# Stick-breaking attention: the second sigmoid written into the SBUF row, the scan in place

## The chip, the cores and the metric

The kernel runs on one core of one Trainium2 chip. The time is that of the whole program on the device, in microseconds; a run gives one number. The kernel before was timed three times: 2722.66 us in the median, 2720.82 and 2723.33 at the ends. The engines are named as in the profile: PE is TensorE (PEld its weight loads), DVE is VectorE, ACT is ScalarE, POOL is GpSimd, SP is SyncE.

## The reference, cut to what matters

The program is a trunk of a gMLP layer, a dense MLP, a stick-breaking attention layer and another dense MLP, all on 1024 tokens of width 1024. The change lies in the attention alone: 16 heads of 64, blocks of 128 queries against all keys up to the block.

```python
z = jnp.einsum('bthd,bshd->bhts', qb, kb).astype(jnp.float32) * scale
log_keep = jnp.where(causal, jax.nn.log_sigmoid(-z), 0.0)
survive = lax.cumsum(log_keep, axis=log_keep.ndim - 1, reverse=True) - log_keep
log_a = jax.nn.log_sigmoid(z) + survive
a = jnp.where(causal, jnp.exp(log_a), 0.0)
outs.append(jnp.einsum('bhts,bshd->bthd', a.astype(vb.dtype), vb))
```

The kernel doesn't go through logarithms. For each row it forms the break b = sigmoid(z) and the keep 1 - b = sigmoid(-z), a running product of the keeps from the right (the "stick"), and a = b times the stick of the key to the right.

## The kernel before, in words

Attention works on tiles: one head, one block of 128 queries, all keys up to it. A head has 8 tiles (`NT`), numbered by `tile_of(k)`, with 128 to 1024 keys. They come in pairs `m` in the order 0, 1, 3, 2, so that the widths of a head's tiles are, in order, 128, 256, 384, 512, 896, 1024, 640, 768. The parity `e` of a tile picks one of two score buffers `z_ps[e]`, each two banks of PSUM. A tile goes through these steps:

- PE, `scores` (lines 1218 and 1220): the scores into `z_ps[e]`, the causal mask added by a last matmul. Before the first of them PE waits for the tile two before, which used the same buffer: `stick_done`.
- ACT, `break_tile` (1608): sigmoid(z) from PSUM into the SBUF row `brk[m][e]`.
- ACT, `keep_tile` (1614): sigmoid(-z), from `z_ps[e]` into `z_ps[e]`, counted by `keep_done`.
- DVE, `sticks` (2084): one scan from right to left, from `z_ps[e]` into the SBUF row `stick[m][e]`, counted by `stick_done`. A scan instruction takes two tensors; the second one is not used in the arithmetic (`ALU.bypass`), and `brk[m][e]` stands in its place.
- POOL, `stick_mult` (894): `brk` times `stick`, both in SBUF, back into `brk`, counted by `a_done`.
- PE, `to_keys` (1235): transposes of `brk`; it waits for `a_done` of both tiles of a pair. ACT (1622) copies them to SBUF as `aT`, and PE, `values` (1248), multiplies with v. ACT (1629) and DVE (2091) split the result in a high and a low part.

Each engine's queue is in order, written out by hand and the same for each head. On PE the scores run two pairs ahead: in step n stand `scores` of tile 2n+4, then the first group of transposes of pair n, a group of `values` of pair n-1, `scores` of tile 2n+5, and the other groups. So the scores of the tile of 640 keys, then of 768 keys, then of 128 keys (of the next head) stand in the queue ahead of the first transposes of the pair of 896 and 1024 keys (line 1235), and the scores of the tile of 256 keys behind them. On ACT the two sigmoids stand between the copies of `aT`. On DVE the scans stand one behind another, with line 2091 once every second pair. POOL has the products alone, and twice in the first two heads a weight split (`w_lo`, line 791, two instructions) between them.

Most of the attention is a hardware loop over two heads. The rest of the program (gMLP, both MLPs, projections) is bound by PE, with high and low parts of fp32 operands split by ACT, DVE and POOL.

Of the kernel before, what the change touches and what calls it, by code (L numbers as in the profile page):

```python
# [22 lines left out]
P = 128  # L23
D = 1024
TOK = 1024
NT = TOK // P
# [144 lines left out]
def wait(eng, sem, value):  # L171

    if isinstance(value, int) and value <= 0:
        return
    eng.wait_ge(sem, value)
# [56 lines left out]
def tile_of(k):  # L232

    m, e = pair(k // 2), k % 2
    return (k // NT) % 2, m, e, 2 * m + e


def build(nc, x, g_mix_pre, g_mix_post, g_ffn_pre, g_ffn_post, w_in, v_g, v_b, w_s, b_s, w_aout,
          w_qkv, w_bout, w1, w2, out):
    ctx = ExitStack()  # L240
    with ctx:
        def sem(name):
            return ctx.enter_context(nc.semaphore(name))
# [4 lines left out]
        def at(name, shape, dt, offset=None):  # L248
            size = 4 if dt != BF16 else 2
            for s in shape[1:]:  # L250
                size *= s
            if offset is None:
                offset = place[0]
                place[0] += -(-size // 32) * 32
                assert place[0] <= 229344, (name, place[0])
            return nc.alloc_sbuf_tensor_at(name, shape, dt, offset=offset)
# [3 lines left out]
        def kb(name, shape, dt, k):  # L260
# [21 lines left out]
                for e in range(2)] for m in range(QP)]  # L282
# [21 lines left out]
        stick = [[at(f"stick{m}{e}", [P, (2 * m + 2) * P + 8], F32, o_stick[m] + e * ((m + 1) * 1024 + 32))  # L304
                  for e in range(2)] for m in range(QP)]
# [50 lines left out]
        z_ps = [psum[:, 2 * b:2 * b + 2, :].rearrange("p a n -> p (a n)") for b in range(2)]  # L356
# [60 lines left out]
        keep_done = sem("keep_done")  # L417
        brk_done = sem("brk_done")
        rows_set = sem("rows_set")
        stick_done = sem("stick_done")  # L420
        a_done = sem("a_done")
# [491 lines left out]
        def _(pe):  # L913
# [293 lines left out]
            def scores(i, k):  # L1207

                hb, _, zb, tb = tile_of(k)
                if tb == 0:  # L1210
                    pe.wait_ge(qk_in[hb], (i + k // (2 * NT)) * (6 * 16) + 6 * 16)
                wait(pe, stick_done, i * (2 * NT) + (k - 1))
                s = (tb + 1) * P
                for c0 in range(0, s, HALF):

                    c1 = c0 + max(2 * P, min(HALF, s - c0))
                    for n in range(2):
                        mm = pe.matmul(z_ps[zb][:, c0:c1], q_st[hb][:, tb * P:(tb + 1) * P], k_st[hb][n][:, c0:c1],  # L1218
                                       start=(n == 0), stop=(n == 1 and c1 < s))
                mm = pe.matmul(z_ps[zb][:, s - P:s], ident_bf[:], mask_bf[:], start=False, stop=True)  # L1220
                mm.then_inc(z_done, 1)
# [31 lines left out]
            def att_step(i):  # L1253
                first, last = isinstance(i, int) and i == 0, isinstance(i, int) and i == HEADS // 2 - 1
                if first:
                    for k in range(4):
                        scores(0, k)
                    pe.wait_ge(rows_set, 2)
                for n in range(2 * QP):
                    more = not (last and n >= 2 * QP - 2)  # L1260
                    if more:
                        scores(i, 2 * n + 4)

                    here = pair(n) + 1
                    before = 0 if first and n == 0 else pair(n - 1) + 1
                    for g in range(max(here, before)):
                        if g < here:
                            to_keys(i, n, g)
                        if g < before:
                            if n:  # L1270
                                values(i, n - 1, g)
                            else:
                                values(i - 1, 2 * QP - 1, g)
                        if more and g == 0:
                            scores(i, 2 * n + 5)
# [25 lines left out]
        def _(act):  # L1301
# [309 lines left out]
            def keep_tile(i, k):  # L1611
                _, m, e, tb = tile_of(k)
                act.wait_ge(brk_done, i * (2 * NT) + (k + 1))
                act.activation(z_ps[e][:, 0:(tb + 1) * P], z_ps[e][:, 0:(tb + 1) * P],  # L1614
                               ACT.Sigmoid, scale=-SCALE).then_inc(keep_done, 1)

            def keys_in(i, n, g):
# [14 lines left out]
            def att_step(i):  # L1632
                first, last = isinstance(i, int) and i == 0, isinstance(i, int) and i == HEADS // 2 - 1
                if first:
                    for k in range(4):
                        break_tile(0, k)
                        keep_tile(0, k)
                    act.wait_ge(qk_out[1], 32 * (2 * D // UC) // 2)
                for n in range(2 * QP):

                    out = None if n % 2 == 0 or (first and n == 1) else (i, n // 2 - 1) if n > 1 else (i - 1, 3)
                    for g in range(4):
                        if not (last and n >= 2 * QP - 2):
                            (break_tile if g % 2 == 0 else keep_tile)(i, 2 * n + 4 + g // 2)
                        if g <= pair(n):
                            keys_in(i, n, g)
                    if out:
                        out_hi(*out)
                    if first and n in (2, 4):
                        hi(U_O + n // 2 - 1, n // 2 - 1)  # L1650
# [13 lines left out]
        def _(dve):  # L1664
# [411 lines left out]
            def sticks(i, k):  # L2076

                _, m, e, tb = tile_of(k)
                dve.wait_ge(keep_done, i * (2 * NT) + (k + 1))
                wait(dve, a_done, i * (2 * NT) + (k - NT + 1))  # L2080
                row = stick[m][e][:, (1 - e) * P:(2 * m + 2) * P][:, ::-1]
                unused = brk[m][e][:, (1 - e) * P:(2 * m + 2) * P]
                keep = z_ps[e][:, 0:(tb + 1) * P][:, ::-1]
                dve.tensor_tensor_scan(row, keep, unused, 1.0, ALU.mult, ALU.bypass).then_inc(stick_done, 1)  # L2084

            def out_lo(i, r):
                h2, g = r // 2, r % 2
# [6 lines left out]
            def att_step(i):  # L2094
                first, last = isinstance(i, int) and i == 0, isinstance(i, int) and i == HEADS // 2 - 1
                if first:
                    for k in range(4):
                        sticks(0, k)
                    dve.wait_ge(qk_out[1], 32 * (2 * D // UC) // 2)
                    ones_column(QP - 1)  # L2100
                    dve.wait_ge(rows_set, 2 + 2 * QP)
                for n in range(2 * QP):
                    more = not (last and n >= 2 * QP - 2)
                    out = None if n % 2 == 0 or (first and n == 1) else (i, n // 2 - 1) if n > 1 else (i - 1, 3)
                    for g in range(4):
                        if more and g % 2 == 0:
                            sticks(i, 2 * n + 4 + g // 2)
                    if out:
                        out_lo(*out)
# [44 lines left out]
```

## Time and profile before

| | |
|---|---|
| median of three runs | 2722.66 us |
| the profiled execution | 2723.14 us |
| its span, first to last instruction | 2721.4 us |
| PE busy over the span | 2543.8 us, 93% |
| DVE, ACT, POOL busy | 1482.9, 1028.4, 1113.1 us |
| mean granted TensorE clock | 0.977 of full speed |
| attention | about 1577 to 1940 us of the span |
| DVE scans, line 2084 | 128, 173.4 us |
| POOL products, line 894 | 128, 153.4 us |

A row of the timeline is: start in us from the span's start, duration in us, engine, line, operation, output<-inputs by the program's names, shape, how many instructions are merged in it, and in brackets the idle time of the engine just before it with what ended it. Where two instructions are merged, the duration is that of both together. Tiles are told apart by their width: 128x896 is the tile of 896 keys. `psum` is both the score buffers and the transposes. A wait is told as "who line <- what it waited for: us in total, times, longest". A row of the windows gives the busy time of each engine in one stretch, the mean granted TensorE clock (1.00 is full speed), and the share of the DMA engines.

### The profile page before, as it was taken

The page shows a single profiled execution, that of the slowest core. Times are in us where ns is not written, and L with a number is a line of the kernel's source. Part 1 is how long each engine was busy: PE and PEld are TensorE (multiplying, and loading weights), DVE is VectorE, ACT ScalarE, POOL GpSimd, SP SyncE. Part 2 cuts the span into 40 slices and gives each one's busy share as a digit, 9 for nine tenths or more (in the row PEclk, how much of TensorE's full clock was granted, in tenths as well). Part 3 has the DMA queues.
Part 4 walks back from the last instruction along what each step waited for, and adds up shares of the span by engine and source line. Part 5 has one row for each costly group of instructions (what it writes and reads, how often), then busy time and mean ns, then how long its engine had stood idle before and what let it go on. Part 6 is the DMA issues. An engine that isn't in the chain of part 4 may idle for free.

```text
span 2721.4 us, 35430 instructions
## 1 busy us (share of the span) xinstructions
PE 2543.8 (93%) x13100; PEld 2152.2 (79%) x13100; DVE 1482.9 (54%) x1959; ACT 1028.4 (38%) x1507; POOL 1113.1 (41%) x716
## 2 busy tenths in 40 slices
PE   7998999998999989999899978888997999989997
PEld 7997888876888868887898857776896888768886
DVE  3214655657656577776311135555348655577775
ACT  5222212234444333334211157777335444333332
POOL 2221221136555465554222144444235555465554
PEclk9999999998999989999999989999999999989999
DMA  5222121142544464443224544334122544464443
GB/s 163 93 92 93 63 70 54 62 133 77 169 151 157 141 229 149 157 171 124 94 93 155 185 116 109 92 92 100 47 80 95 171 151 147 163 231 139 139 166 120
DMA packets 180417, 342.56 MB, mean 126 GB/s; under 512 B 12224, under 2 KB 95168, under 8 KB 178240
## 3 DMA queue, kind: packets, MB, share of 16 engines
q1 hardware_dynamic: 173632, 311.47, 35.0%
q10 hardware_dynamic: 6656, 29.36, 2.7%
q8 instruction: 82, 1.34, 0.2%
q14 instruction: 47, 0.39, 0.0%
HBM read 235.95 MB, written 104.86 MB: 125 GB/s over the span
## 4 chain that ended last, share of the span: by engine, by line
PE 81%; DVE 7%; ACT 4%; issue 4%; POOL 3%; DMA 2%; SPq 0%; ACTq 0%; DVEq 0%; POOLq 0%
PE psum L1117 22%; PE psum L1160 20%; PE psum L934 13%; PE psum L921 12%; PE psum L945 5%; PE psum L1248 3%; DVE stick L2084 2%; PE psum L1218 2%; PE psum L1235 2%; ACT psum L1614 1%; PE psum L1038 1%; ACT brk L1608 1%; POOL rw_lo L878 1%; DMA a_raw<-a_forms 1%; DVE acc L1691 1%
## 5 line engine op out<-in xcount | busy, mean ns | idle before, releaser
L1160 PE MATMUL psum<-rw_hi,ra_hi 128*128 128x512 f32 x896 | 353.8, 395 | 17.4 <-POOL rw_lo L878 8.9
L1160 PE MATMUL psum<-rw_lo,ra_hi 128*128 128x512 f32 x896 | 352.1, 393 | 0.0
L1160 PE MATMUL psum<-rw_hi,ra_lo 128*128 128x512 f32 x896 | 351.6, 392 | 0.0
L791 POOL TENSOR_TENSOR w_lo<-stage,w_hi 128x1024 fp32r<-128x1024 f32 x56 | 134.2, 2419 | 507.5 <-ACT w_hi L1305 507.5
L878 POOL TENSOR_TENSOR rw_lo<-blk,rw_hi 128x512 fp32r<-128x512 f32 x160 | 239.7, 1528 | 196.1 <-ACT rw_hi L1446 196.0
L2084 DVE TENSOR_TENSOR_SCAN stick<-psum,brk 128x128 f32<-128x128 f32 (+7 forms) x128 | 173.4, 1356 | 161.2 <-ACT psum L1614 159.7
L894 POOL TENSOR_TENSOR brk<-brk,stick 128x128 f32<-128x128 f32 (+7 forms) x128 | 153.4, 1208 | 222.2 <-DVE stick L2084 208.6
L1441 ACT ACTIVATE ra_hi<-a_raw 128x2048 fp32r<-128x2048 f32 x56 | 107.3, 1917 | 357.7 <-PE psum L1160 259.4
L1971 DVE TENSOR_TENSOR ra_lo<-a_raw,ra_hi 128x512 fp32r<-128x512 f32 x224 | 230.9, 1040 | 19.9 <-ACT ra_hi L1441 19.9
L934 PE MATMUL psum<-w_hi,hT_hi 128*128 128x256 f32 x768 | 219.8, 286 | 1.4 <-DVE hT_lo L2091 1.4
L934 PE MATMUL psum<-w_lo,hT_hi 128*128 128x256 f32 x768 | 218.6, 285 | 0.0
L934 PE MATMUL psum<-w_hi,hT_lo 128*128 128x256 f32 x768 | 218.6, 285 | 0.0
L1160 PEld LDWEIGHTS psum<-rw_hi,ra_hi 128*128 128x128 f32 x896 | 170.3, 190 | 56.1 <-POOL rw_lo L878 11.7
L1987 DVE TENSOR_TENSOR acc<-psum,acc 128x512 f32<-128x512 f32 x192 | 131.9, 688 | 140.8 <-PE psum L1160 140.8
L1160 PEld LDWEIGHTS psum<-rw_hi,ra_lo 128*128 128x128 f32 x896 | 170.2, 190 | 36.1
L1160 PEld LDWEIGHTS psum<-rw_lo,ra_hi 128*128 128x128 f32 x896 | 170.4, 190 | 35.3
L1248 PE MATMUL psum<-aT,v_st 128*128 128x256 f32 x640 | 161.6, 384 | 0.0
L1218 PE MATMUL psum<-k_st,q_st 128*128 128x512 f32 (+2 forms) x384 | 112.8, 404 | 49.9 <-DVE stick L2084 44.4
L934 PEld LDWEIGHTS psum<-w_hi,hT_hi 128*128 128x128 f32 x768 | 149.0, 194 | 1.9 <-DVE hT_lo L2091 1.8
L934 PEld LDWEIGHTS psum<-w_lo,hT_hi 128*128 128x128 f32 x768 | 149.0, 194 | 0.0
L934 PEld LDWEIGHTS psum<-w_hi,hT_lo 128*128 128x128 f32 x768 | 148.7, 194 | 0.0
L791 POOL TENSOR_TENSOR wq_lo<-stage_q,wq_hi 128x1024 fp32r<-128x1024 f32 x24 | 57.9, 2436 | 193.5 <-ACT wq_hi L1305 193.5
(225 smaller groups left out, 6402.4 us busy)
## 6 DMA issues: line engine op xcount, KB each, us to landing
a_raw<-a_forms SPq DMA_DIRECT2D x56, 1024.0 KB, 5.5
a_forms<-a_out SPq DMA_DIRECT2D x64, 512.0 KB, 3.1
blk<-mlp_w_in SPq DMA_DIRECT2D x32, 1024.0 KB, 5.4
a_forms<-a_out SPq DMA_DIRECT2D x32, 768.0 KB, 3.3
stage<-a_w_in_in SPq DMA_DIRECT2D x16, 1024.0 KB, 5.4
stage<-mlp_w_in SPq DMA_DIRECT2D x16, 1024.0 KB, 6.0
raw<-mlp_w_in SPq DMA_DIRECT2D x32, 512.0 KB, 5.3
x_res<-xt SPq DMA_DIRECT2D x24, 512.0 KB, 4.9
```

The lines of the kernel that those rows point to most:

```text
L791: pool.tensor_tensor(w[b][1][:, c], raw[:, c], w[b][0][:, c].bitcast(F32), ALU.subtract).then_inc(unit_ready, 1)
L878: ins = pool.tensor_tensor(w[1][:, k, :], src[:, k, :], w[0][:, k, :].bitcast(F32), ALU.subtract)
L894: pool.tensor_tensor(brk[m][e][:, c0:c1], brk[m][e][:, c0:c1], stick[m][e][:, c0 + 1:c1 + 1], ALU.mult).then_inc(a_done, 1)
L921: mm = pe.matmul(psum[:, bank, :], w[ub][sw][:, k * UC + f * P:k * UC + (f + 1) * P], h[sh][:, k, half * HALF:(half + 1) * HALF], start=(n ...
L934: mm = pe.matmul(psum[:, bank, c0:c0 + UC], h[sh][:, k, t * P:(t + 1) * P], w[ub][sw][:, k * UC:(k + 1) * UC], start=(n == 0), stop=(n == ...
L945: mm = pe.matmul(psum[:, 4 + j % 4, :], a_buf[ab][sa][:, r, t * P:(t + 1) * P], wt[ub][sw][:, r * D + n2 * HALF:r * D + (n2 + 1) * HALF], ...
L1117: mm = pe.matmul(psum[:, bank, :], W[p][sw][:, k, :], H[layer][p][sh][:, k, :], start=(p in (1, 2, 5) and n == 0), stop=(p in (4, 2, 3) an ...
L1160: mm = pe.matmul(psum[:, down_bank(n, tp), :], ring_a[n % 3][sa][:, k, tp * P:(tp + 1) * P], ring_w[n % 3][sw][:, k, :], start=(p in (1, 2 ...
L1218: mm = pe.matmul(z_ps[zb][:, c0:c1], q_st[hb][:, tb * P:(tb + 1) * P], k_st[hb][n][:, c0:c1], start=(n == 0), stop=(n == 1 and c1 < s))
L1248: mm = pe.matmul(psum[:, 6 + m // 2, (m % 2) * 2 * P:(m % 2 + 1) * 2 * P], v_st[hb][:, 2 * m + 1 - p, :], aT[n % 2][:, p * 2 * P:(p + 1) * ...
L1971: ins = dve.tensor_tensor(ring_a[n % 3][1][:, k, :], a_raw[n % 2][:, k, :], ring_a[n % 3][0][:, k, :].bitcast(F32), ALU.subtract)
L2084: dve.tensor_tensor_scan(row, keep, unused, 1.0, ALU.mult, ALU.bypass).then_inc(stick_done, 1)
```

## The change

```diff
@@ PE, scores @@
-                wait(pe, stick_done, i * (2 * NT) + (k - 1))
+                wait(pe, keep_done, i * (2 * NT) + (k - 1))
@@ ACT, keep_tile @@
                 act.wait_ge(brk_done, i * (2 * NT) + (k + 1))
-                act.activation(z_ps[e][:, 0:(tb + 1) * P], z_ps[e][:, 0:(tb + 1) * P],
+                wait(act, a_done, i * (2 * NT) + (k - NT + 1))
+                act.activation(stick[m][e][:, (1 - e) * P:(2 * m + 2) * P], z_ps[e][:, 0:(tb + 1) * P],
                                ACT.Sigmoid, scale=-SCALE).then_inc(keep_done, 1)
@@ DVE, sticks @@
                 dve.wait_ge(keep_done, i * (2 * NT) + (k + 1))
-                wait(dve, a_done, i * (2 * NT) + (k - NT + 1))
                 row = stick[m][e][:, (1 - e) * P:(2 * m + 2) * P][:, ::-1]
                 unused = brk[m][e][:, (1 - e) * P:(2 * m + 2) * P]
-                keep = z_ps[e][:, 0:(tb + 1) * P][:, ::-1]
-                dve.tensor_tensor_scan(row, keep, unused, 1.0, ALU.mult, ALU.bypass).then_inc(stick_done, 1)
+                dve.tensor_tensor_scan(row, row, unused, 1.0, ALU.mult, ALU.bypass).then_inc(stick_done, 1)
```

The second sigmoid goes from PSUM to the row `stick[m][e]` in SBUF, and the scan reads and writes that row. The next scores into the same PSUM buffer wait for that sigmoid. The wait that keeps a stick row from being overwritten before its product has read it (`a_done` of the tile 8 earlier) stands on ACT instead of DVE. The number of scans, sigmoids, products and matmuls and their order on each engine are as before. Both inputs of the scan are now SBUF tensors (`stick` and the unused `brk`); before, the first was PSUM.

No instruction that computes moves; the sequence on ACT in the loop is the one place where rows are added, and it shows in its queue (the names are those of the tiles above; brackets give the semaphores waited for):

```order
 L1608 ACTIVATE brk_78<-psum 128x896 [waits aT_psum,z_done]
-L1622 ACTIVATE aT_98<-psum 128x384 [waits av_done,aT_psum]
-L1614 ACTIVATE psum<-psum 128x896 [waits brk_done]
+L1623 ACTIVATE aT_98<-psum 128x384 [waits av_done,aT_psum]
+L1615 ACTIVATE stick_106<-psum 128x896 [waits a_done,brk_done]
 L1608 ACTIVATE brk_79<-psum 128x1024 [waits aT_psum,z_done]
-L1614 ACTIVATE psum<-psum 128x1024 [waits brk_done]
+L1615 ACTIVATE stick_107<-psum 128x1024 [waits a_done,brk_done]
```

That is ACT's queue outside the hardware loop, around the two widest tiles; the line numbers behind the edit are one higher on ACT. The second sigmoid stands where it stood, with another destination and a second semaphore. Inside the loop seven of the sixteen second sigmoids get a register instruction of their own in front for the second semaphore.

## Rows read from the trace of the kernel before

**Rows 1.** Waits in the attention, 1577 to 1940 us: who, line, for what.
```profile
PE psum L1218 <- DVE stick L2084: 44.4, 53, 2.5
...
PE psum L1235 <- POOL brk L894: 6.1, 4, 2.3
```
**Rows 2.** Timeline of one head, PE, ACT, DVE and POOL.
```profile
1706.65 0.23 PE L1220 MATMUL psum<-mask_bf,ident_bf 128*128 128x128 bf16 x1
...
1706.86 4.45 DVE L2084 TENSOR_TENSOR_SCAN stick<-psum,brk 128x896 f32<-128x896 f32 x2 [1.75 <-ACT psum L1614]
...
1707.97 1.01 ACT L1614 ACTIVATE psum<-psum 128x1024 f32<-128x1024 f32 x1
...
1709.03 1.78 POOL L894 TENSOR_TENSOR brk<-brk,stick 128x896 f32<-128x896 f32 x1 [3.25 <-DVE stick L2084]
...
1711.45 3.29 POOL L894 TENSOR_TENSOR brk<-brk,stick 128x1024 f32<-128x1024 f32 x2 [0.65 <-DVE stick L2084]
1711.73 1.49 DVE L2084 TENSOR_TENSOR_SCAN stick<-psum,brk 128x640 f32<-128x640 f32 x1 [0.42 <-ACT psum L1614]
...
1713.27 0.50 PE L1218 MATMUL psum<-k_st,q_st 128*128 128x256 f32 x2 [0.43 <-DVE stick L2084]
...
1713.68 0.50 PE L1235 MATMUL psum<-ident,brk 128*128 128x128 f32 x3
...
1714.02 1.03 PE L1248 MATMUL psum<-aT,v_st 128*128 128x256 f32 x4
1714.21 0.80 ACT L1614 ACTIVATE psum<-psum 128x768 f32<-128x768 f32 x1
...
1715.04 1.76 DVE L2084 TENSOR_TENSOR_SCAN stick<-psum,brk 128x768 f32<-128x768 f32 x1 [1.82 <-ACT psum L1614]
...
1716.85 0.50 PE L1218 MATMUL psum<-k_st,q_st 128*128 128x256 f32 x2 [1.80 <-DVE stick L2084]
...
1719.86 0.54 PE L1235 MATMUL psum<-ident,brk 128*128 128x128 f32 x3
```
**Rows 3.** The same view, the end of the next head's widest scores.
```profile
1728.12 0.23 PE L1220 MATMUL psum<-mask_bf,ident_bf 128*128 128x128 bf16 x1
```
**Rows 4.** Timeline of DVE and POOL in the first MLP.
```profile
806.04 0.68 DVE L1898 TENSOR_TENSOR s<-raw 128x512 f32<-128x512 f32 x1
806.22 1.66 POOL L838 TENSOR_TENSOR wu_1lo<-raw,wu_1hi 128x512 fp32r<-128x512 f32 x1 [1.46 <-ACT wu_1hi L1357]
806.86 1.57 DVE L1898 TENSOR_TENSOR s<-s,raw 128x512 f32<-128x512 f32 x1
808.94 1.28 POOL L838 TENSOR_TENSOR wu_5lo<-s,wu_5hi 128x512 fp32r<-128x512 f32 x1 [1.06 <-ACT wu_5hi L1357]
```
**Rows 5.** Timeline of POOL and DVE in the last MLP.
```profile
2631.69 3.00 POOL L878 TENSOR_TENSOR rw_lo<-blk,rw_hi 128x512 fp32r<-128x512 f32 x2 [4.94 <-ACT rw_hi L1446]
...
2632.11 1.42 DVE L1971 TENSOR_TENSOR ra_lo<-a_raw,ra_hi 128x512 fp32r<-128x512 f32 x1
```
**Rows 6.** The page's costliest groups: two DVE lines, out<-in, busy, mean ns.
```profile
L1971 DVE TENSOR_TENSOR ra_lo<-a_raw,ra_hi 128x512 fp32r<-128x512 f32 x224 | 230.9, 1040 | 19.9 <-ACT ra_hi L1441 19.9
...
L1987 DVE TENSOR_TENSOR acc<-psum,acc 128x512 f32<-128x512 f32 x192 | 131.9, 688 | 140.8 <-PE psum L1160 140.8
```
**Rows 7.** Groups by shape in the attention, columns as in rows 6.
```profile
L894 POOL TENSOR_TENSOR brk<-brk,stick 128x1024 f32<-128x1024 f32 x16 | 32.1, 2005 | 9.0 <-DVE stick L2084 9.0
...
L894 POOL TENSOR_TENSOR brk<-brk,stick 128x768 f32<-128x768 f32 x16 | 24.8, 1547 | 34.0 <-DVE stick L2084 34.0
...
L791 POOL TENSOR_TENSOR w_lo<-stage,w_hi 128x1024 fp32r<-128x1024 f32 x4 | 9.4, 2362 | 8.9 <-ACT w_hi L1305 8.9
```
**Rows 8.** Windows: us, PE, PEld, DVE, ACT, POOL busy, PE clock, DMA share.
```profile
1620.00:1630.00 10.00, 4.18 (x20) 3.30 (x18) 4.25 (x4) 4.49 (x9) 10.00 (x6) 0.73 1.04 238
1700.00:1740.00 40.00, 34.53 (x198) 27.43 (x197) 23.46 (x19) 28.09 (x51) 18.34 (x15) 1.00 0.37 93
```
**Rows 9.** Timeline, PE's longest stall in the attention.
```profile
1624.69 0.79 PE L1218 MATMUL psum<-k_st,q_st 128*128 128x256 f32 x2 [3.54 <-DMA k_st<-qk_lo]
```

## The prediction

> **What bounds the kernel now.** I read first the page, by which PE is busy in 93% of the span, then the waits of the attention stretch, then the timeline of one head. PE stands 44.4 us before new scores because the scan of the tile two earlier still holds their PSUM buffer (53 times, at most 2.5 us); it stands only 6.1 us in all, four times, for a product before transposes [rows 1]. POOL's own waits for scans cost nothing as long as PE doesn't wait for POOL. In steady state (1700 to 1740 us) PE is busy 34.5 of 40 us at full clock [rows 8], so what is there to win lies in those stalls.
>
> I count one head from T0, the end of the mask matmul of the tile with 1024 keys: 1706.65 + 0.23 = 1706.88. The next head's T0 is 1728.12 + 0.23 = 1728.35 [rows 2, 3]. The period is 21.47 us. In it PE runs, after T0:
>
> - the scores of 128 keys at 6.39 (1713.27), a stall of 0.43 before them;
> - the first transposes of the pair 896/1024, line 1235, at 6.80 (1713.68). They need the product of 1024, which POOL runs from 4.57 (1711.45) for 2.00: to 6.57. They are late by next to nothing, but there is only 0.2 us of room;
> - the scores of 256 keys at 9.97 (1716.85), after the period's one large stall, 1.80: PE was free at 8.17 (1714.02 + 1.03) and the scan of 768 ended at 9.92 (1715.04 + 1.76);
> - the first transposes of the pair 640/768 at 12.98 (1719.86), 3.01 after those scores began, and from there without a stall 8.49 us to the next T0.
>
> All from [rows 2, 3].
>
> **The change part by part.** *PE's wait.* The large stall goes: the second sigmoid of 768 ends at 8.13 (1714.21 + 0.80) [rows 2], 1.8 us before its scan. The scores of 256 can start as soon as PE gets there. If nothing else moved, the chain keep 1024 (ready at 2.10) - scan to 4.43 - product to 6.57 would hold the transposes at about 6.6, the scores of 256 would start 1.40 later, and the next head would come 1.75 us sooner. That is what the edit gives if it is only a wait.
>
> *The scan's operands.* They are not only a wait. The scan now reads two SBUF tensors, and beside it runs a POOL product that reads two as well. Two elementwise instructions like that exclude each other in this trace. At 806.22 POOL starts while DVE works from SBUF until 806.72; it takes 1.66 us, where the same instruction alone takes 1.28, and ends at 807.88. DVE's next one starts at 806.86 and takes 1.57 where 0.68 is usual: it ends 0.55 after POOL [rows 4]. In the last MLP a DVE instruction that arrives during the first of two POOL ones takes 1.42: it is done 0.56 after that one ends (2631.69 + 1.28), before the second goes on, so a waiting DVE instruction gets in between two of POOL [rows 5]. Over the whole run the DVE line with two SBUF inputs has a mean of 1040 ns, the one of equal size with one input in PSUM 688 [rows 6]. In the attention of before the scans have PSUM on one side, and the product of 896 runs its 1.78 us right beside a scan with nothing lost on either [rows 2]. So each crossing costs: the held one ends its own duration less 0.12 us after the other (0.13 on DVE) [rows 4].
>
> The Trainium skill states the same as a rule (SBUF — State Buffer, Who interferes with whom): a DVE instruction with two SBUF inputs contends with a GpSimd one that reads SBUF, with an exclusive lock for the whole instruction. It names elementwise ones; whether a scan counts no row here shows, as none of before has both inputs in SBUF. By the rule it does, and the sum is the one worked out below; without it the sum would be the 1.75 us gained.
>
> I take the elementwise rows for the scan too, and walk one head again, from T0. The scans of 896 and 1024 run as before, to 4.43: 1024 is asked for at 2.13, the product of 896 at 2.15 [rows 2]; if the product came first the end of the chain would be the same. The product of 896 (1.78) is held until 4.43 and ends at 4.43 + 1.66 = 6.09. The scan of 640 (1.49) is asked for at 4.85 now (1711.73 [rows 2]), hardly later after the change; it waits, and goes in between: 6.09 + 1.36 = 7.45. The product of 1024 (2.00 [rows 7]): 7.45 + 1.88 = 9.33. The transposes follow at about 9.43, where they were at 6.80: 2.63 us later. PE has been out of work since the scores of 128, which now end at about 6.1: a stall of 3.3 us.
>
> From there the scores of 256 start 1.40 later, at 10.83 (they were at 9.97). DVE and POOL meanwhile: scan of 768, 9.33 + 1.63 = 10.96; product of 640 (1.3, from the 3.29 for it and that of 1024), to 12.15; scan of 128 (0.42: scans grow by 0.27 with each 128 keys, 1.49 to 1.76), which waited for it, to 12.45; product of 768 (1.55), 12.45 + 1.43 = 13.88 [rows 2, 7]. PE reaches its transposes at 10.83 + 3.01 = 13.84, so they go at 13.98, and T0 of the next head is 13.98 + 8.49 = 22.47. The period grows by 1.00 us: a gain of 1.75 turned into a loss of 1.00.
>
> *Bounds of that.* From below, only the part of an instruction that grows with its width excludes: 2.1 ns an element for scans (1.76 less 1.49 over 128), 1.8 for products (2005 less 1547 over 256 [rows 7]); 2560 and 1920 elements in the chain give 8.8 us, transposes at 8.9, +0.5 a head. From above, full durations and 0.15 us from each release to the start (the product of 896 begins 0.15 after its scan [rows 2]): 2.02 + 2.29 + 1.78 + 1.49 + 2.00 + 0.6 = 10.2, +1.8 a head. I take 1.0, the walk with the measured handovers.
>
> *What else moves.* The second sigmoid into SBUF instead of PSUM: the first sigmoid does just that, at the same widths and the same pace; 0. Its added wait, for the product eight tiles back, and the register rows: that product ended most of a head ago even in the walk, and the aT copies, which already have such a row in front, start without a gap; 0. Should it bind, behind it on ACT stand the aT copies, for which values on PE wait. A scan from SBUF against one from PSUM: the two-SBUF elementwise 0.68 [rows 4] against 0.69 for the PSUM one [rows 6]; 0. The skill's table (VectorE: DVE Perf Modes, The TRN2 errata) has 58 fixed cycles from SBUF and 120 from PSUM, which would shorten each of three scans in the chain by 65 ns, an estimate of 3 us over 16 heads; this trace shows no such difference, and the measurement decides.
>
> *The sum.* Of the 16 heads all but the first two and the last are steady: 13 at +1.0. The last head has no scores to pull forward behind it: its product of 768 ends 2.4 us later, +2.5. In the first two, POOL has two weight splits of 2.36 us each [rows 7] between products, which now exclude scans as well: a scan gets in between the two splits and another behind them, of 384 and 512 keys the first time, of 640 and 768 the second, about 2 and 3 us that the products behind come later (an estimate from the scans' durations). Against it stand about 3 us of stalls on scans that go there. +2. In all +17.5 us on the profiled execution's 2723.14 (span 2721.4 and 1.7 around it): 2740.6. It lies 0.5 above the median, so 2740.
>
> **The rivals.**
> 1. *The scan does not exclude POOL.* It consumes one element in two DVE cycles, unlike the elementwise ones, and nothing of before has this form. Then only the wait counts: 13 periods at -1.75, some -4 at the ends, 2696. It decides if a scan and a product of 1024 keep 2.29 and 2.00 side by side. This is the case not slower than before. Against it: only the operands' place told the two kinds apart in [rows 4 to 6]. Chance 0.12.
> 2. *They share, each slowed in part.* A scan leaves every second read to POOL, the product of 1024 comes at about 8 instead of 9.33, and gain and loss cancel: transposes at 8.0, scores of 256 at 9.4, then -0.5 a head with the ends against it: about 2720. Chance 0.06.
> 3. *The clock falls as well.* After a PE stall of 3.54 us [rows 9] the granted clock of the stretch is 0.73 [rows 8], that is 5.4 of 10 us at the low level of 1.2 GHz, 2.7 us of full speed lost; the stalls of at most 2.5 us in steady state leave it at 1.00. My walk makes a stall of 3.3 us once a head. If each of 14 drops the clock: 2740 + 38 = 2778; if some do, between. Chance 0.08.
>
> **How the numbers follow.** The forecast has 0.74; its bounds give 13 x 0.5 + 4 = +10 and 13 x 1.8 + 8 = +31, so its own range is 2731 to 2756. To hold 8 in 10 I go down to 2721, which takes in the sharing case, and up to 2766 for a few drops of the clock; out are rival 1 and the upper end of 3. No change, within 0.2% (5.4 us, about what a measurement here can tell), gets 0.07, faster 0.12, slower 0.81.
>
> **What would show it.** Right: scans of 2.3 us and products of 2.0 us whose recorded durations reach 3 to 4 us when they overlap; a new wait of PE line 1235 for POOL line 894 of some 3 us a head, about 45 us in all in place of 6.1, while PE's wait of 44.4 us for the scan is gone and what comes for the sigmoid is small; period 22.5. Wrong: scan and product means as before and a period under 20 us (rival 1), or a clock below 1.00 in the steady stretch (rival 3).

## The result, and the profile after

The changed kernel takes 2765.32 us (median of 4, 2762.49 to 2765.69), the kernel before 2722.99 us in its 4 runs; the ratio is 1.0151, with an interval of 1.0135 to 1.0167. It is slower by 42 us, where 17.5 were forecast: the time lies inside the wide range of the prediction (2721 to 2766), at its upper end, and outside the forecast's own (2731 to 2756). The profiled execution took 2762.49 us, span 2760.8, mean clock 0.965; against the profile before that is 39.4 us, and the accounts below are of these.

The waits of the attention in the changed kernel, where [rows 1] stood before (the scan's line is now 2083, the second sigmoid's 1615):

```profile
PE psum L1235 <- POOL brk L894: 71.8, 17, 7.9
...
PE psum L1218 <- ACT stick L1615: 4.0, 2, 2.0
```

PE's 44.4 us before the scores are gone, as the edit says; 4.0 are left. In their place PE stands 71.8 us before the transposes of line 1235, in 17 waits: in each steady head one of 3.95 to 4.10 us, for the product of 1024 keys. The groups by shape (before, in the same order: 1.78 and 1.76 us in [rows 2], 2005 ns in [rows 7], 1.49 us in [rows 2]):

```profile
L894 POOL TENSOR_TENSOR brk<-brk,stick 128x896 f32<-128x896 f32 x16 | 58.7, 3671 | 51.7 <-DVE stick L2083 51.7
L2083 DVE TENSOR_TENSOR_SCAN stick<-stick,brk 128x768 f32<-128x768 f32 x16 | 55.7, 3483 | 0.2
L894 POOL TENSOR_TENSOR brk<-brk,stick 128x1024 f32<-128x1024 f32 x16 | 49.5, 3094 | 2.3 <-DVE stick L2083 2.3
L2083 DVE TENSOR_TENSOR_SCAN stick<-stick,brk 128x640 f32<-128x640 f32 x16 | 45.8, 2865 | 1.1 <-ACT stick L1615 1.1
```

The second number behind the bar is the mean: the instruction is held by another engine, and its record counts the holding as work. One head of the timeline, counted as in [rows 2] from T0 = 1718.16 + 0.23 = 1718.39 (merged instructions have their common end):

```profile
1718.16 0.23 PE L1220 MATMUL psum<-mask_bf,ident_bf 128*128 128x128 bf16 x1
...
1718.23 1.95 PE L1248 MATMUL psum<-aT,v_st 128*128 128x256 f32 x8
...
1718.37 4.46 DVE L2083 TENSOR_TENSOR_SCAN stick<-stick,brk 128x896 f32<-128x896 f32 x2 [1.69 <-ACT stick L1615]
...
1720.54 3.86 POOL L894 TENSOR_TENSOR brk<-brk,stick 128x896 f32<-128x896 f32 x1 [3.34 <-DVE stick L2083]
1720.54 7.00 POOL L894 TENSOR_TENSOR brk<-brk,stick 128x896 f32<-128x896 f32 x2 [3.34 <-DVE stick L2083]
...
1723.42 0.23 PE L1220 MATMUL psum<-mask_bf,ident_bf 128*128 128x128 bf16 x1
...
1725.67 3.48 DVE L2083 TENSOR_TENSOR_SCAN stick<-stick,brk 128x768 f32<-128x768 f32 x1
...
1727.67 0.54 PE L1235 MATMUL psum<-ident,brk 128*128 128x128 f32 x3 [4.02 <-POOL brk L894]
1728.05 1.24 PE L1248 MATMUL psum<-aT,v_st 128*128 128x256 f32 x4
1728.73 0.99 PE L1218 MATMUL psum<-k_st,q_st 128*128 128x256 f32 x2
1729.52 0.33 PE L1220 MATMUL psum<-mask_bf,ident_bf 128*128 128x128 bf16 x1
...
1730.49 1.85 PE L1248 MATMUL psum<-aT,v_st 128*128 128x256 f32 x4
```

The product of 896 is held until its neighbour's scan has ended (4.44 after T0) and ends at 6.01; the scan of 640 goes in between; the product of 1024 ends at 9.15, and the transposes start at 9.28. PE had its last work at 5.26 and stands 4.02 us. Behind the stall the same matmuls are slower than elsewhere: four of line 1248 take 1.24 and 1.85 us against 1.03, the mask matmul 0.33 against 0.23. Two windows behind the stall (columns as in [rows 8]), and then windows of one head each, from one head's first sigmoid of 1024 keys to the next head's: the first two heads of the attention, and two steady ones:

```profile
1727.67:1731.67 4.00, 4.00 (x17) 3.56 (x18) 2.88 (x3) 1.53 (x4) 4.00 (x2) 0.63 1.02 212
1731.67:1735.67 4.00, 4.00 (x27) 3.19 (x27) 1.00 (x2) 2.51 (x6) 1.23 (x3) 0.94 0.01 2
```
```profile
1587.43:1617.93 30.50, 23.40 (x101) 18.85 (x102) 20.35 (x10) 16.35 (x29) 20.18 (x10) 0.75 0.18 52
1617.93:1647.55 29.62, 20.74 (x109) 17.26 (x109) 13.92 (x9) 17.09 (x29) 17.02 (x10) 0.80 0.48 107
...
1718.43:1742.02 23.59, 19.57 (x109) 16.51 (x109) 15.55 (x10) 15.40 (x28) 14.32 (x8) 0.93 0.38 89
1742.02:1766.29 24.27, 20.20 (x109) 17.10 (x109) 15.58 (x11) 15.51 (x28) 14.31 (x8) 0.86 0.37 86
```

The same windows of the kernel before, for its first two heads and one steady one:

```profile
1588.85:1615.22 26.37, 19.90 (x101) 16.23 (x102) 11.74 (x10) 16.44 (x29) 14.16 (x10) 0.84 0.09 28
1615.22:1642.33 27.11, 20.62 (x109) 16.80 (x109) 11.60 (x10) 17.31 (x30) 14.11 (x10) 0.87 0.64 149
...
1706.92:1728.39 21.47, 18.78 (x109) 14.98 (x109) 11.97 (x10) 15.28 (x28) 9.58 (x8) 1.00 0.41 98
```

Before, all 13 steady heads are at 1.00. After, none is: nine are at 0.93, four at 0.86. A share of 0.07 off 23.6 us is 1.65 us of full speed lost, which in these numbers is a clock that stands at the lower level (1.2 of 2.4 GHz) for 3.3 us, right behind the stall. In the four heads at 0.86 it is about twice that (3.4 us of full speed lost).

### The profile page after: what moved, and what is told of

It reads as the page before. It is cut to its first block, busy times and chain, and to the rows that moved or that the text cites. A ratio compares the mean times of both kernels' runs of the same rounds, so it can differ in the third digit from the quotient of the medians.

```text
span 2760.8 us, 35430 instructions
## 1 busy us (share of the span) xinstructions
PE 2559.6 (93%) x13100; PEld 2178.4 (79%) x13100; DVE 1543.4 (56%) x1959; ACT 1029.7 (37%) x1507; POOL 1185.7 (43%) x716
## 4 chain that ended last, share of the span: by engine, by line
PE 79%; POOL 5%; DVE 5%; issue 5%; ACT 3%; DMA 2%; SPq 0%; ACTq 0%; POOLq 0%; DVEq 0%
PE psum L1117 21%; PE psum L1160 20%; PE psum L934 13%; PE psum L921 12%; PE psum L945 5%; PE psum L1248 4%; POOL brk L894 3%; PE psum L1235 2%; DVE stick L2083 1%; PE psum L1038 1%; PE psum L1218 1%; POOL rw_lo L878 1%; DMA a_raw<-a_forms 1%; DVE acc L1692 1%; ACT stick L1615 1%
## 5 line engine op out<-in xcount | busy, mean ns | idle before, releaser
L2083 DVE TENSOR_TENSOR_SCAN stick<-stick,brk 128x128 f32<-128x128 f32 (+7 forms) x128 | 232.6, 1837 | 138.5 <-ACT stick L1615 136.0
L894 POOL TENSOR_TENSOR brk<-brk,stick 128x128 f32<-128x128 f32 (+7 forms) x128 | 224.0, 1769 | 185.1 <-DVE stick L2083 148.6
L1248 PE MATMUL psum<-aT,v_st 128*128 128x256 f32 x640 | 181.2, 419 | 0.0
L1235 PE MATMUL psum<-ident,brk 128*128 128x128 f32 x576 | 99.5, 300 | 72.1 <-POOL brk L894 71.8
```

Source lines behind the costliest of these rows:

```text
L894: pool.tensor_tensor(brk[m][e][:, c0:c1], brk[m][e][:, c0:c1], stick[m][e][:, c0 + 1:c1 + 1], ALU.mult).then_inc(a_done, 1)
L1235: mm = pe.transpose(psum[:, 4 + gi % 2, at_col:at_col + P], brk[m][e][:, col:col + P], ident[:])
L1248: mm = pe.matmul(psum[:, 6 + m // 2, (m % 2) * 2 * P:(m % 2 + 1) * 2 * P], v_st[hb][:, 2 * m + 1 - p, :], aT[n % 2][:, p * 2 * P:(p + 1) * ...
L2083: dve.tensor_tensor_scan(row, row, unused, 1.0, ALU.mult, ALU.bypass).then_inc(stick_done, 1)
```

## The experiments

Each experiment was timed beside the kernel before, which took 2723.43 us beside e1 to e4, 2725.85 beside e5 to e8 and 2727.13 beside e9. Ratios are to it, with their intervals; medians of different groups can differ by these 4 us for nothing. Because the totals hold the clock's share too, *clean heads* are compared beside them: steady heads whose window has a clock of 1.00.

| kernel | median us | ratio | clean head, us | steady heads below clock 0.99, of 13 |
|---|---|---|---|---|
| before | 2722.99 | | 21.47 to 21.56 | 0 |
| changed | 2765.32 | 1.0151 (1.0135 to 1.0167) | none | 13 |
| e1 no shared input | 2693.94 | 0.9890 (0.9874 to 0.9907) | 19.37 to 19.55 | 0 |
| e2 old wait | 2757.58 | 1.0125 (1.0108 to 1.0142) | 22.33 to 22.40 | 10 |
| e3 24 filler matmuls | 2753.75 | 1.0115 (1.0095 to 1.0136) | 22.06, 22.13 | 11 |
| e4 PSUM second input, old wait | 2731.62 | 1.0026 (1.0016 to 1.0035) | 21.50 to 21.58 | 6 |
| e5 60 filler matmuls | 2737.61 | 1.0040 (1.0026 to 1.0054) | 22.06 to 22.21 | 0 |
| e6 products on DVE | 2703.84 | 0.9915 (0.9898 to 0.9931) | 20.38 to 20.61 | 0 |
| e7 the same, on the kernel before | 2736.21 | 1.0033 (1.0021 to 1.0046) | 22.38 to 22.57 | 3 |
| e8 only the scan of 640 freed | 2741.09 | 1.0043 (1.0026 to 1.0060) | none | 13 |
| e9 e1 and the product of 1024 in two halves | 2690.18 | 0.9866 (0.9840 to 0.9891) | 19.16 to 19.26 | 0 |

**e1: the scans of 1024, 640 and 768 keys get an unused second input that is not in SBUF.** Everything else is the changed kernel; two waits keep the PSUM cells whose value is read (and not used) from being written meanwhile. The five other scans of a head keep both inputs in SBUF.

```diff
+                one = {5: psum[:, 7, 0:1], 6: z_ps[0][:, HALF:HALF + 1], 7: z_ps[1][:, HALF:HALF + 1]}.get(k % NT)
+                if one is not None:
+                    unused = one.to_broadcast([P, (tb + 1) * P])
```

> The changed kernel, with the unused second input of the scans of 1024, 640 and 768 keys taken from a PSUM bank that is idle then (one value, broadcast), so that these scans have one SBUF input; the PE wait stays on the second sigmoid, the scan stays in place. Theory A (a scan with two SBUF inputs and a POOL product exclude each other, and the late product of 1024 keys then starves PE until its clock falls): products of 896, 1024, 640 keys back to 1.8, 2.0, 1.3 us; no PE stall over 1 us in steady state, clock 1.00 there, period about 19.7 us, total about 2696 us (2690 to 2704). Rival B (the loss comes from the second sigmoid's new place, the in-place scan or the new wait, not from the ports): all of these are still in, so the total stays near 2762.

The groups by shape of e1:

```profile
L2090 DVE TENSOR_TENSOR_SCAN stick<-stick,psum 128x1024 f32<-128x1024 f32 x16 | 36.6, 2286 | 5.0 <-ACT stick L1615 2.8 <-PE psum L1248 2.0
...
L894 POOL TENSOR_TENSOR brk<-brk,stick 128x1024 f32<-128x1024 f32 x16 | 32.0, 1999 | 10.7 <-DVE stick L2090 10.7
L894 POOL TENSOR_TENSOR brk<-brk,stick 128x896 f32<-128x896 f32 x16 | 28.4, 1774 | 51.7 <-DVE stick L2090 51.7
...
L2090 DVE TENSOR_TENSOR_SCAN stick<-stick,psum 128x640 f32<-128x640 f32 x16 | 23.4, 1463 | 0.7 <-ACT stick L1615 0.7
...
L2090 DVE TENSOR_TENSOR_SCAN stick<-stick,brk 128x128 f32<-128x128 f32 x16 | 19.5, 1218 | 6.8 <-ACT stick L1615 6.6
```

The product of 896 is back from 3671 to 1774 ns, that of 1024 from 3094 to 1999, the scan of 640 from 2865 to 1463. The scan of 128 keys, left with both inputs in SBUF, is still held, by the product of 768: 1218 ns, where it took 415 before. The time is 2693.94, and the head is 19.49 us, near the expected 19.7; a stall of 1.54 to 1.63 us before the transposes is left in each steady head, where none over 1 us was expected. Since a value that is never used decides it, the exclusion hangs on where the scan's second operand lies, and the loss of the changed kernel comes from it, directly and through the clock. The head is 2.0 us shorter than before: that is what the freed wait is worth.

**e2: the changed kernel with the old wait of PE for the scan.**

```diff
-                wait(pe, keep_done, i * (2 * NT) + (k - 1))
+                wait(pe, stick_done, i * (2 * NT) + (k - 1))
```

> The changed kernel with PE's scores waiting for the scan again (stick_done), everything else as changed. Theory A: exclusion is still there, product of 1024 still late, first transposes of 896/1024 at about 9.4 us after T0, but PE's idle time is spread in front of three scores as well, no single stall is long enough for the clock to fall: clock 1.00 in steady state, period about 22.5 us, total about 2740 (2733 to 2750), so faster than the changed kernel by about 20 us. Rival C (the loss is made by the wait that was moved, since PE runs ahead and then stands): total back at 2723. Rival D (the clock has no part, the whole loss is handover time): no change from 2762 or slower.

It came out at 2757.58, outside the 2733 to 2750 that were expected: the clock was to hold and fell in ten heads. The rival by which the moved wait makes the loss (back to 2723) is out all the same. The waits and one head on PE:

```profile
PE psum L1218 <- DVE stick L2083: 36.8, 48, 2.6
...
PE psum L1235 <- POOL brk L894: 29.6, 17, 6.6
```
```profile
1723.82 0.51 PE L1218 MATMUL psum<-k_st,q_st 128*128 128x256 f32 x2 [1.43 <-DVE stick L2083]
...
1725.69 0.90 PE L1235 MATMUL psum<-ident,brk 128*128 128x128 f32 x3 [1.29 <-POOL brk L894]
1726.38 1.92 PE L1248 MATMUL psum<-aT,v_st 128*128 128x256 f32 x4
```

Here PE's idle time comes in two pieces of 1.43 and 1.29 us, the score matmuls between them still at full pace, and yet the clock is low behind the second (1.92 for the four matmuls of line 1248). Together they are 2.72 us within 3.30. Three heads escaped, at 22.33 to 22.40. So with the exclusion in place, the old wait costs a clean head only 0.2 us over the new one (22.16, e5): the freed wait is worth almost nothing there, because the product is what PE waits for.

**e3 and e5: matmuls that keep PE at work in the stall.** Ahead of the first transposes of the pair 896/1024 stand 24 (e3) or 60 (e5) bf16 matmuls of 128x128 into PSUM cells that nothing reads then.

```diff
+                    if more and pair(n) == QP - 1:
+                        for _ in range(60):
+                            pe.matmul(z_ps[0][:, HALF:HALF + P], ident_bf[:], mask_bf[:], start=True, stop=True)
```

> The changed kernel with 24 small bf16 matmuls of PE (128x128 of constants into an idle PSUM bank) once a head, in front of the first transposes of the pair 896/1024, where PE stands 4 us; their result is used nowhere. Theory A with the clock as second term: the stall is still bounded by the product of 1024 keys (9.3 us after T0), but its idle part is cut to about 2 us and the clock stays at 1.00: period about 22.5 instead of 23.6, total about 2748 (2743 to 2754). Rival D (the clock has no part): the same 2762 or, with the added work, a little more.

> As e3_filler, with 60 small matmuls instead of 24, about 3.7 us of them (24 took 1.5 us), so PE has next to no idle time in front of the first transposes of the pair 896/1024. The handovers between scans and products are untouched. Theory A with the clock as second term: the clock is 1.00 in steady state, every head takes the 22.1 us that the few undisturbed heads of e3_filler took (22.06 and 22.13), total about 2740 (2736 to 2745): some 22 us of the changed kernel's loss is clock, some 17 are handovers. Rival D (the clock has no part): 2762 or more.

PE in one head of e3, then of e5:

```profile
1720.46 1.50 PE L1266 MATMUL psum<-mask_bf,ident_bf 128*128 128x128 bf16 x24
...
1724.64 0.54 PE L1235 MATMUL psum<-ident,brk 128*128 128x128 f32 x3 [2.68 <-POOL brk L894]
1725.02 1.42 PE L1248 MATMUL psum<-aT,v_st 128*128 128x256 f32 x4
```
```profile
1711.48 3.51 PE L1266 MATMUL psum<-mask_bf,ident_bf 128*128 128x128 bf16 x60
...
1715.67 0.54 PE L1235 MATMUL psum<-ident,brk 128*128 128x128 f32 x3 [0.68 <-POOL brk L894]
1716.05 1.03 PE L1248 MATMUL psum<-aT,v_st 128*128 128x256 f32 x4
```

A stall of 2.68 us is left in e3, and the clock still falls in 11 of 13 heads. Its 2753.75 lies inside the expected 2743 to 2754 by luck, as the clock was expected to hold. With 0.68 left, in e5, it falls in none, and the kernel takes 2737.61, as expected: 28 us less than the changed kernel, for 900 matmuls more. The products and scans are held as long as before (product of 896 3802 ns, scan of 640 2962). So what the filler gives back, 28 us of the 42, is clock, and the rival by which the clock has no part (2762 or more) is out. The 11.8 us left by the medians of e5's own comparison (7 to 15 by the interval) are the handovers and all else, and not quite free of the clock: the last head, without filler, still has a stall of 4.25 us and a clock of 0.85.

**e4: a second operand in PSUM and the old wait.** That is the kernel before, but for where the second sigmoid writes, the added wait on ACT, and the scan that runs in place, with its PSUM operand as the second.

```diff
-                wait(pe, keep_done, i * (2 * NT) + (k - 1))
+                wait(pe, stick_done, i * (2 * NT) + (k - 1))
...
-                unused = brk[m][e][:, (1 - e) * P:(2 * m + 2) * P]
+                unused = z_ps[e][:, 0:(tb + 1) * P]
```

> The changed kernel (second sigmoid into the SBUF row, scan in place, the added wait on ACT), but the scan's unused second input is the score buffer in PSUM, and PE waits for the scan again, as it must then. One SBUF input a scan. Theory A: no exclusion, the waits of before: the time of before, 2723 (2719 to 2727), scan and product durations as before. Rival B (new place of the sigmoid, in-place scan, wait on ACT cost time): some 10 to 40 us slower than before.

Scan and product of 1024 are at 2285 and 1998 ns, here with the second operand read from PSUM in its full width, and seven steady heads at 21.50 to 21.58, as before. So the sigmoid into SBUF and the scan from SBUF cost nothing. The total, 2731.62, is 8 us higher all the same and outside the expected 2719 to 2727, by a ratio of 1.0026 (1.0016 to 1.0035), since in six heads the clock fell behind a stall that is there in every head. Two heads in a row, on PE:

```profile
1669.45 0.50 PE L1218 MATMUL psum<-k_st,q_st 128*128 128x256 f32 x2 [1.83 <-DVE stick L2083]
...
1670.30 1.03 PE L1248 MATMUL psum<-aT,v_st 128*128 128x256 f32 x4
...
1691.03 0.50 PE L1218 MATMUL psum<-k_st,q_st 128*128 128x256 f32 x2 [1.82 <-DVE stick L2083]
...
1692.28 1.92 PE L1248 MATMUL psum<-aT,v_st 128*128 128x256 f32 x4
```

The stalls are alike within 0.01 us, and one head keeps its clock and the other not; it costs 1.65 us each time. The kernel before has the same stall (1.80 in [rows 2] and in every other head, 1.62 in the heads between) and kept the clock in all 13 heads of its profile. What makes the difference stays open.

**e6 and e7: the products on DVE, behind each scan,** from the changed kernel (e6) and from the kernel before (e7). POOL is busy for 0.00 us from 1660 to 1900 us in both, so no scan there meets a POOL instruction.

```diff
+                dve.wait_ge(stick_done, i * (2 * NT) + (k + 1))
+                dve.tensor_tensor(brk[m][e][:, c0:c1], brk[m][e][:, c0:c1], stick[m][e][:, c0 + 1:c1 + 1],
+                                  ALU.mult).then_inc(a_done, 1)
```

> The changed kernel with every product moved from POOL to DVE, right behind its scan. DVE can't exclude itself, and POOL has no products. Theory A: the new wait is worth its gain without the exclusion, DVE is busy some 18 us a head: first transposes of 896/1024 at about 6.8 us after T0, those of 640/768 at about 11.8, period about 20.2, total about 2705 (2698 to 2715). Rival B (the second sigmoid's place, the in-place scan or the new wait cost the time): over 2740.

> The kernel before (second sigmoid in PSUM, PE waits for the scan) with every product moved to DVE behind its scan: the partner of e6_products_on_dve, so that the two show what the change is worth where no exclusion is possible. The scan of 768 keys now stands behind two more products on DVE, so the scores of 256 keys wait longer: at about 10.8 us after T0 where they were at 9.97; period about 22.3, clock drops possible, total about 2735 (2728 to 2755). Theory A: e6 lies some 30 us below e7. Rival B: e6 above e7.

2703.84 and 2736.21, both as expected: with the exclusion taken away in quite another manner the freed wait brings 32 us (2.0 us a clean head), as between e4 and e1 (38 us, 2.0 a clean head; part of the 38 is e4's clock). With the exclusion it costs 8 (e2 to the changed kernel, by the totals, which hold the clock's share).

**e8: only the scan of 640 keys gets the PSUM operand.** It is the one that goes in between the two products.

> The changed kernel with only the scan of 640 keys freed of its second SBUF input (one value of an idle PSUM bank instead). It takes one of the two links out of the chain scan 1024 - product 896 - scan 640 - product 1024: the product of 1024 then ends at about 8.0 us after T0 instead of 9.2, the period is 21.0 at full clock, with a PE stall of about 2.9 us that may still cost 1.5 us of clock a head: total between 2722 and 2745, under the changed kernel in any case. If the scans' place in the chain did not matter and only the number of exclusions did (five of eight scans crossed by a product), one scan less would give a quarter or less of the 70 us between e1_no_shared_input and the changed kernel: about 2745 or more.

2741.09, inside the expected 2722 to 2745. The group of the product that was overtaken, which stood at 3094 ns:

```profile
L894 POOL TENSOR_TENSOR brk<-brk,stick 128x1024 f32<-128x1024 f32 x16 | 31.9, 1993 | 0.0
```

Nothing stands between the two products now, and in a head with T0 at 1710.58 the transposes start at 1718.67, 8.09 after it: 1.19 earlier than in the changed kernel, near the 1.36 that the walk had for this scan. The stall is still 2.84 us, and the clock falls in all 13 heads. The held scan of 640 is so worth 24 us by itself, and to free it alone does not bring the kernel back to before.

**e9: e1, and the product of 1024 in two halves,** the right half first, so that the first transposes can start after it; the last group waits for the whole.

```diff
+                if k % NT == 5:
+                    mid = 4 * P
+                    pool.tensor_tensor(brk[m][e][:, mid:c1], brk[m][e][:, mid:c1], stick[m][e][:, mid + 1:c1 + 1],
+                                       ALU.mult).then_inc(a_right, 1)
+                    c1 = mid
```

> e1_no_shared_input with the product of 1024 keys cut in two on POOL, the right half of the row first; the first transposes of the pair 896/1024 wait for that half alone, the third group for the whole. In e1_no_shared_input PE waited 1.5 us a head there, for the whole product. If the product's latency is what bounds e1: the transposes come 0.9 us sooner, the product behind it 0.1 to 0.2 later, period 18.7 to 19.0 instead of 19.5, total about 2685 (2680 to 2690). If the wait only moves (to the transposes of 640/768, whose product of 768 keys comes 0.15 later): 2692 to 2696.

2690.18, between the two expectations. In e1 a wait of 1.54 to 1.63 us for the product of 1024 was left in each steady head. The waits of e1, then of e9, where the transposes have line 1244, line 897 is the right half and line 900 every other product:

```profile
PE psum L1235 <- POOL brk L894: 30.9, 18, 4.1
```
```profile
PE psum L1244 <- POOL brk L900: 9.5, 16, 3.1
PE psum L1244 <- POOL brk L897: 8.0, 12, 0.7
```

13.4 of 30.9 us go, and the head shrinks by only 0.25 (19.49 to 19.24), 3 us in all: part of the wait moved to the next pair's transposes, whose product now starts no sooner. By their intervals e9 and e1 can't be told apart; both beat the kernel before by over 1%.

## Why the prediction was right in kind and short in size

**The scan excludes POOL's product: right.** The central step, taken over from elementwise instructions, held to 0.2 us at each point of the walk: end of the product of 896 at 6.01 after T0 (forecast 6.09), start of the transposes 9.28 (9.43), end of the scan of 768 at 10.76 (10.96). A scan that arrives while a product runs does go in between that one and the next. The Trainium skill's rule on two SBUF inputs (SBUF — State Buffer, Who interferes with whom), which was cited with the doubt whether a scan counts, agrees with this trace: it counts, with 3671 ns against e1's 1774 for the product of 896 keys. Rival 1 (2696) is what e1 does, not what the change does, and rival 2, sharing, is out by the same rows: whoever comes second ends nearly its whole duration after the first.

**The freed wait: right.** 44.4 us of waits became 4.0, and without the exclusion they are worth 2.0 us a head (forecast 1.75). **The operands' other costs, taken at nothing: right,** by e4's clean heads. The added waits on ACT show in no row of the waits: the second sigmoid (line 1615) never stands for a product.

**The net loss per head by handovers: right in sign, 0.65 where 1.00 stood.** In e5, where the clock is whole, the transposes stand at 9.28, the scores of 256 keys at 10.33 (forecast 10.83), the next transposes at 13.63 (13.98), the period is 22.16 (22.47). The scores follow the transposes by 1.05 us, not 1.40: the walk added the recorded durations of matmuls that overlap in the records.

**The failed step is the clock.** The sum put the clock at nothing. The prediction said that "the stalls of at most 2.5 us in steady state leave it at 1.00" and gave the fall of the clock, after its own stall of 3.3 us, a chance of 0.08. It came in every head, and cost 21.7 us over the 13 steady ones. The reading itself was off: the wait of 2.5 us in [rows 1] lies in the first head, and the longest in the steady heads of before is 1.80. The account of the 39.4 us between the profiled executions, from the starts of the sigmoid of 1024 keys:

| part | forecast | measured | from |
|---|---|---|---|
| 13 steady heads, handovers | +13.0 | +8.3 | sum of e5's 288.06 less before's 279.74 |
| 13 steady heads, clock | 0 | +21.7 | sum 309.79 of the changed kernel less e5's 288.06 |
| first two heads | +2 | +6.6 | 60.12 less 53.48; 53.62 in e5 |
| last head and what follows | +2.5 | +4.1 | the rest |
| up to the first such sigmoid | 0 | -1.4 | 1587.43 less 1588.85 |

In the first two heads it is mostly the clock again: the windows' 0.75 and 0.80 against 0.84 and 0.87 are 13.5 us of full speed lost against 7.7. e5 has them at 53.62, next to before's 53.48, but with a clock of 0.93 and 0.94, better than before's, so that its handovers there are hidden by the clock that it gained. So nearly all that the sum lacks is one term. The price that rival 3 gave it, 2.7 us a head, was high: it is 1.67 in the mean, 1.4 to 1.5 over e5's 22.16 in the nine heads at 0.93 and 2.1 to 2.2 in the four at 0.86. The window from which the price was read, 1620 to 1630 us in [rows 8], has a second stall in it, 2.28 us before line 1235, beside the one of 3.54.

Two things led there. The stall itself came out at 4.02 instead of 3.3, because PE was out of work at 5.26 and not at 6.1. Before, the three scores behind T0 stood behind small waits of 0.27, 0.18 and 0.43 us; the last work ended at 6.97 (1713.62 + 0.23), and 6.97 less these 0.88 gives the 6.1. The scores of 640 and 768 keys and the mask matmul of 128, before, and then the scores of all three after:

```profile
1708.94 0.97 PE L1218 MATMUL psum<-k_st,q_st 128*128 128x512 f32 x4 [0.27 <-DVE stick L2084]
...
1711.36 0.96 PE L1218 MATMUL psum<-k_st,q_st 128*128 128x512 f32 x4 [0.18 <-DVE stick L2084]
...
1713.62 0.23 PE L1220 MATMUL psum<-mask_bf,ident_bf 128*128 128x128 bf16 x1
```
```profile
1719.83 1.04 PE L1218 MATMUL psum<-k_st,q_st 128*128 128x512 f32 x4
...
1721.78 1.05 PE L1218 MATMUL psum<-k_st,q_st 128*128 128x512 f32 x4
...
1723.10 0.48 PE L1218 MATMUL psum<-k_st,q_st 128*128 128x256 f32 x2
```

With those of 128 keys (1713.27 in [rows 2]) they start at 2.06, 4.48 and 6.39 after T0 before, and at 1.44, 3.39 and 4.71 after: 1.68 us sooner and not 0.88, since the records of matmuls that nothing holds overlap (1719.83 lies before the end of the values at 1718.23 + 1.95), and those behind a wait do not. It is the same slip as with the 1.40 above: PE runs further ahead of the chain that it then has to wait for. And the level at which the clock holds was read off from one kernel in which the stalls lay elsewhere; e2 lost it behind stalls of 1.43 and 1.29 us close together, and e4 behind one of 1.82. A stall longer than any of the steady stretch should have carried a large chance of losing the clock, not a small one.

**What stays open.** Why e4 loses the clock in some heads behind the stall that the kernel before has as well, while e1 keeps it in all 13 with stalls of 1.54 us. The 4.1 us behind the last such sigmoid can be placed, though not split by cause. From that sigmoid to the end of the last values, before and then after:

```profile
1922.07:1941.16 19.09, 16.52 (x91) 13.30 (x90) 8.77 (x6) 10.52 (x17) 6.61 (x4) 1.00 0.00 0
```
```profile
1957.34:1980.10 22.76, 18.17 (x91) 15.15 (x90) 11.85 (x6) 10.77 (x17) 11.23 (x4) 0.85 0.00 0
```

So 3.7 of the 4.1 lie in the last head, with a stall of 4.25 us and a clock of 0.85 in it; no experiment put a filler there.

## What to carry to other kernels

An operand that is read and not used still costs its way in: before a VectorE instruction gets both inputs in SBUF, look which GpSimd work runs beside it, walk the handovers one by one, and if there is any, point the unused operand at PSUM (here those few lines, with two waits that protect the cells, turned +1.5% into -1.1%). When a wait of TensorE is removed, ask where its idle time gathers next: many small stalls that become one large one can cost the clock, and that was here more than the handovers. When clocks differ between variants, compare single periods with a granted clock of 1.00 before comparing totals.

## What was not expected of the hardware

- A scan with two SBUF inputs is shut out by, and shuts out, a GpSimd product for the whole instruction, though the second input has no part in the arithmetic; a single PSUM value broadcast along the row frees it (scan of 640: 2865 to 1463 ns).
- The granted clock fell behind a TensorE stall of 1.82 us (e4), and behind two of 1.43 and 1.29 us close together (e2), in some heads and not in others with equal stalls; in e4 each fall cost 1.65 us of a 21.5 us head.
- 60 useless bf16 matmuls in each stall (3.51 us, TensorE busy instead of idle) made the changed kernel 28 us faster, with the handovers as long as before.
